# A gelu written out: tanh on the scalar engine, its argument and last factor on the vector engine

## The reference, cut to what matters

```
def peer_ffn(h, w_q, sub_keys, u_tab, v_tab):
    # q = h @ w_q; scores against the sub keys; top 16 of each half, top 16 of their sums
    cv, ci = lax.top_k(cand, 16)                  # for each token and each of 8 heads
    gates = jax.nn.softmax(cv, axis=-1)           # 128 factors a token
    def chunk_fn(xc, ic, gc):                     # 128 tokens
        uc, vc = take(u_tab, ic), take(v_tab, ic) # 128 rows of 1024 for each token
        act = jax.nn.gelu(einsum('cd,ckd->ck', xc, uc))   # the tanh form
        return einsum('ck,ckd->cd', gc * act, vc)
```

## Time and profile before

| | |
|---|---|
| median of 3 runs | 2805.45 us (2803.26 to 2807.54) |
| profiled execution, own time | 2803.49 us |
| its span on the core | 2801.3 us |
| busy: PE, DVE, ACT, POOL | 90%, 49%, 23%, 18% |
| chain that ended last, by engine | PE 55%, DMA 22%, DVE 9%, SP's queue 7%, ACT 5% |
| DVE line L1939, dots | 512 instructions, 612.1 us busy, 202.8 us idle before them |
| ACT line L1452, gelu | 256 instructions, 52.2 us; 52 table loads, 66.7 us |
| ACT line L1443, softmax exponentials | 31 table loads, 39.8 us |
| DVE line L1950, coefficients | 256 instructions, 56.0 us; 184.4 us idle before them |

### The profile page before, as it was taken

One profiled execution on the slowest core, in us unless ns is written; L12 is line 12 of the kernel. 1 busy time (PEld: TensorE's weight loads), 2 busy tenths in 40 slices (PEclk: granted clock), 3 DMA queues, 4 the chain that ended last, 5 costly groups with the idle time before them and its releaser, 6 DMA issues.

```text
span 2801.3 us, 31076 instructions
## 1 busy us (share of the span) xinstructions
PE 2531.6 (90%) x10682; PEld 1293.7 (46%) x10682; DVE 1365.7 (49%) x3708; ACT 643.4 (23%) x1475; POOL 494.7 (18%) x534
## 2 busy tenths in 40 slices
PE   9899999999999998998987889889899799798876
PEld 6644444443343343996443334336444346333332
DVE  2312222212212213556677776775675665678753
ACT  0310100101001001231222242442332542332212
POOL 1000000000000000002333332232322222333330
PEclk9989999999999999999999999999999999999999
DMA  7479999999999998458999999999999989999994
GB/s 248 195 295 415 418 416 418 419 416 418 418 417 418 419 417 332 151 211 325 420 421 421 421 419 384 419 368 418 420 418 417 408 334 418 406 398 422 422 421 168
DMA packets 179718, 1058.04 MB, mean 378 GB/s; under 512 B 18816, under 2 KB 19240, under 8 KB 81312
## 3 DMA queue, kind: packets, MB, share of 16 engines
q0 software_dynamic: 75104, 540.07, 47.1%
q1 hardware_dynamic: 104512, 516.71, 45.9%
HBM read 1055.64 MB, written 2.63 MB: 378 GB/s over the span
## 4 chain that ended last, share of the span: by engine, by line
PE 55%; DMA 22%; DVE 9%; SPq 7%; ACT 5%; issue 2%; POOL 0%; DVEq 0%; ACTq 0%; POOLq 0%
PE ps L1093 17%; DMA big<-in_uv,small 15%; PE ps L704 14%; DMA big<-in_w_gate_up 7%; PE ps L817 5%; SPq L434 4%; PE ps L694 3%; SPq L426 3%; PE ps L910 3%; DVE big L1939 3%; PE ps L1045 2%; PE ps L926 2%; PE ps L739 2%; PE ps L560 1%; ACT L1452 1%
## 5 line engine op out<-in xcount | busy, mean ns | idle before, releaser
L1093 PE MATMUL ps<-big,small 128*128 128x512 f32 x2048 | 993.8, 635 | 201.1 <-ACT small L1457 201.1
L2078 POOL DMA_INDIRECT big<-in_uv,small x512 | 484.1, 946 | 2209.1 <-DVE small L1919 1230.8
L1093 PEld LDWEIGHTS ps<-big,small 128*128 128x128 f32 x2048 | 401.4, 203 | 740.4 <-issue 452.2
L704 PE MATMUL ps<-big 128*64 128x512 f32 x3072 | 705.7, 601 | 22.8 <-DMA big<-in_w_gate_up 19.5
L1939 DVE SCALAR_TENSOR_TENSOR big<-big,ps 128x1024 f32<-128x1024 f32 x512 | 612.1, 1217 | 202.8 <-DMA big<-in_uv,small 202.6
L704 PEld LDWEIGHTS ps<-big 128*64 128x64 f32 x3072 | 203.6, 137 | 418.5 <-issue 337.9
L1457 ACT ACTIVATE small<-con,small 128x128 f32<-128x128 f32 x512 | 177.6, 394 | 311.1 <-DVE small L1950 309.2
L1687 DVE COPY big<-ps 128x512 f32<-128x512 f32 x32 | 22.1, 692 | 418.8 <-PE ps L704 418.8
L1673 DVE TENSOR_TENSOR big<-ps,big 128x256 f32<-128x256 f32 x64 | 27.2, 425 | 309.2 <-PE ps L721 309.2
L1452 ACT ACTIVATE small<-small 128x2 f32<-128x2 f32 x256 | 52.2, 204 | 528.5 <-DVE big L1939 520.7
L817 PEld LDWEIGHTS ps<-hT,ring 128*128 128x128 f32 x1280 | 146.2, 192 | 8.6 <-issue 7.2
(11 more groups left out here) (299 smaller groups left out, 1950.7 us busy)
## 6 DMA issues: line engine op xcount, KB each, us to landing
big<-in_w_gate_up SPq DMA_DIRECT2D x256, 1024.0 KB, 20.2
big<-in_w_down SPq DMA_DIRECT2D x128, 1024.0 KB, 23.1
ring<-in_peer_w_q SPq DMA_DIRECT2D x48, 512.0 KB
ring<-in_w_kv SPq DMA_DIRECT2D x22, 512.0 KB
ring<-in_w_in SPq DMA_DIRECT2D x16, 512.0 KB
ring<-in_a_w_in SPq DMA_DIRECT2D x16, 512.0 KB
big<-in_uv,small POOLq DMA_INDIRECT x512
ring<-in_ple_w_gate SPq DMA_DIRECT2D x16, 512.0 KB
```

The lines of the kernel that those rows point to most:

```text
L704: last = pe.matmul(ps[side * CAP:(side + 1) * CAP, bank + b, :], o, w[:, at:at + BANK], start=start, stop=stop, skip_group_check=True)
L1093: last = pe.matmul(ps[:, out_bank(f) + z, :], diagonal(k), rows(k)[:, D + z * BANK:D + (z + 1) * BANK], start=(k % PHASE == 0), stop=((k + ...
L2078: pool.indirect_dma_start(out=rows(k), out_offset=None, in_=io[f"uv{n // UNITS}"], in_offset=bass.IndirectOffsetOnAxis(ap=rows_at[:, at:at ...
```

## The change

The gelu's instruction on ACT becomes a tanh with scale sqrt(2/pi) on an argument that DVE prepares. DVE, after the two dots of the share, computes `g_cube` = 0.044715 d * d and `g_arg` = (g_cube + 1) * d, and signals `dots_ready` after that; for these it waits for its own dots. After `gelu_ready` it computes `g_twice` = (tanh + 1) * d and then the coefficient from it. The factor 0.5 goes into `p_rec`, in one more small instruction per head. Three small tiles are added in free columns of `small`; they aren't doubled, one set serves all shares. Nothing else changes, no transfer and no PE instruction.

```diff
--- before.py
+++ after.py
@@ -346,6 +346,7 @@
         pick = small[:, 784:912].bitcast(BF16)
         i12, e_row = small[:, 912:944], small[:, 944:960]
         p_sum, p_rec, p_nmax = (small[:, 960 + k * UNITS:960 + (k + 1) * UNITS] for k in range(3))
+        g_cube, g_arg, g_twice = (small[:, 1008 + k * SHARE:1008 + (k + 1) * SHARE] for k in range(3))
         cv = small[:, 1024:1024 + PICKS]
         rows_at = small[:, 1280:1280 + PICKS].bitcast(U32)
         dots, acts, coef = (small[:, 1536 + k * PICKS:1536 + (k + 1) * PICKS] for k in range(3))
@@ -1449,7 +1450,7 @@
                 k = n * SHARE
                 act.wait_ge(S["dots_ready"], n + 1)
                 at = slice(k % PICKS, k % PICKS + SHARE)
-                act.activation(acts[:, at], dots[:, at], ACT.Gelu_apprx_tanh).then_inc(S["gelu_ready"], 1)
+                act.activation(acts[:, at], g_arg, ACT.Tanh, scale=float(np.sqrt(2 / np.pi))).then_inc(S["gelu_ready"], 1)
                 act.wait_ge(S["coef_ready"], n + 1)
                 for k in range(n * SHARE, (n + 1) * SHARE):
                     if k >= DIAGS:
@@ -1938,16 +1939,21 @@
                     r = rows(k)[:, 0:D]
                     ins = dve.scalar_tensor_tensor(r, r, 1.0, tok, op0=ALU.mult, op1=ALU.mult,
                                                    accum_out=dots[:, k % PICKS:k % PICKS + 1])
-                ins.then_inc(S["dots_ready"], 1)
+                link(ins)
+                at = slice(n * SHARE % PICKS, n * SHARE % PICKS + SHARE)
+                link(dve.scalar_tensor_tensor(g_cube, dots[:, at], 0.044715, dots[:, at], op0=ALU.mult, op1=ALU.mult))
+                dve.scalar_tensor_tensor(g_arg, g_cube, 1.0, dots[:, at], op0=ALU.add, op1=ALU.mult)\
+                    .then_inc(S["dots_ready"], 1)
                 u16 = u % UNITS
                 if t % SHARES == 0:
                     dve.wait_ge(S["cv_exp"], u + 1)
                     link(dve.reciprocal(p_rec[:, u16:u16 + 1], p_sum[:, u16:u16 + 1]))
+                    link(dve.tensor_scalar(p_rec[:, u16:u16 + 1], p_rec[:, u16:u16 + 1], 0.5, None, ALU.mult))
                 for which, piece in chosen(f, t):
                     choose(which, piece)
-                at = slice(n * SHARE % PICKS, n * SHARE % PICKS + SHARE)
                 dve.wait_ge(S["gelu_ready"], n + 1)
-                dve.scalar_tensor_tensor(coef[:, at], acts[:, at], p_rec[:, u16:u16 + 1], cv[:, at],
+                link(dve.scalar_tensor_tensor(g_twice, acts[:, at], 1.0, dots[:, at], op0=ALU.add, op1=ALU.mult))
+                dve.scalar_tensor_tensor(coef[:, at], g_twice, p_rec[:, u16:u16 + 1], cv[:, at],
                                          op0=ALU.mult, op1=ALU.mult).then_inc(S["coef_ready"], 1)
 
             mask2 = triu.unsqueeze(1).broadcast_to((P, 4, P))
```

## The result

| | us, median | ratio, 95% interval |
|---|---|---|
| before (20 runs) | 2805.15 | |
| after (20 runs) | 2810.99 | 1.0023 (1.0017 to 1.0030) |

The change makes the kernel 5.8 us slower by the medians, 6.5 us (4.8 to 8.4) by the ratio, just more than the 0.2% that the prediction set as its bound. The profiled execution of after has a span of 2811.5 us against 2801.3, so the two traces differ by more than the medians do. The size of the whole change is taken from the medians, that of each experiment from its ratio; the traces are read for where things lie.

A forecast was written before the change was run, and what follows sets the result against it. DMA transfers were taken as the bound, with time to win or lose only in dips: first heads -4.1, second heads -2.9, last-phase start +3.1, tail +0.6, together -3.3 us, giving 2802.1 us against the median, range 2789 to 2814.

The forecast's parts named there:

- stretch C: Up to the third dip (2480 to 2510 us), at the change to the last phase: added DVE steps cost +3.1 us.
- the tail: End of the kernel: the last share is on the path, +0.6 us.
- full share: A share (two gathered rows) whose dots are on the path pays all three added DVE steps, 0.63 us.
- The load at 2486.82: Table load after a sigmoid in the last-phase dip: counted as 0 gained, 1.28 us as the other end.
- The drain: Skill page's further 1380 ns per table switch; not counted, since the chain's row shows 1.29 us in all.
- the heads' term: Attention heads of both token tiles, where transfers dip: loads removed (10.2 and 6.4 us) outweigh added DVE steps.
- short shares: Shares where DVE waits for ACT anyway pay only the second factor behind the tanh, 0.21 us.
- The loads' term: Thirteen table loads on the path in the two tiles' heads go, worth 10.2 and 6.4 us, 16.6 in all.
- The rest hidden: Outside the dips full transfers hide added DVE work; thinnest from 2500 to 2660 us, by 0.25 us a share.
- The list of dips: Where DMA engines are not full: 1820 to 1880 us (8.7 us), 2220 to 2300 (16.3), 2480 to 2510 (3.6).
- DVE as the bound: Rival, last phase: a share costs DVE more than the transfers' 4.98 us; time 2819, chance 0.17.
- The clock: Rival, head dips: shorter idles keep TensorE's clock up, giving back 12 us at most; 2796 at half, chance 0.22.

The follow-up runs named there:

- tanh_only: Kernel before with the gelu replaced by a tanh of the dots, nothing added on DVE; 2791.56 against 2803.78 us, ratio 0.9954.
- heads_only: Kernel before with the written-out gelu only in ticks 22 to 39 of phases 1 and 2, half in the identity; 2802.30 us, ratio 0.9995.
- tanh_heads: Kernel before with a plain tanh of the dots, no DVE steps, only in ticks 22 to 39 of phases 1 and 2; 2793.56 us, ratio 0.9963.
- dve_only: Changed kernel with the gelu back on ACT and all of DVE's added steps kept; 2820.88 us, ratio 1.0056 to the kernel before.
- last_only: Kernel before with the written-out gelu only in the last phase (f = 3), half in the identity; 2808.03 against 2803.78 us, ratio 1.0011.
- first_only: Kernel before with the written-out gelu only in phase 0, half in the identity; 2805.21 us, ratio 1.0002.
- rest_only: Kernel before with the written-out gelu in phase 0 and in phases 1 and 2 outside ticks 22 to 39; 2807.53 us, ratio 1.0013.
- mixed: Tanh throughout, argument on ACT in ticks with search work and no logarithm, otherwise on DVE with last product beside the tanh; 2804.43 us, ratio 1.0001 to before.
- heads_mixed: Kernel before with that mixed form only in ticks 22 to 39 of phases 1 and 2; 2800.53 us, ratio 0.9989.
- all_shadow: Changed kernel with the dots' product made during the tanh and the half in the identity; 2804.86 us, ratio 1.0004 to the kernel before.

## Why the prediction was wrong, point by point

- **The direction.** Forecast were 3.3 us less, measured were 5.8 more. The time lies in the range (2789 to 2814), but the sign is wrong. Of the rivals none came as written. Of the 9.1 us between the two, 7.1 are in the heads and 2.1 in the part held to be hidden; stretch C and the tail came 0.6 under the sum.
- **Prices.** A step of 0.21 us (measured 0.20), a full share of 0.63 (0.59), the tanh at the gelu's 204 ns, at least 60 loads gone (66 at these two lines, 10 more at the chain's exponentials): right. "Below 0.17 nothing small lies" was a misreading: before has 32 steps of 128x1 at L1900, of 0.154 us each, and the new ones take 0.154 to 0.164; it changes nothing, since a linked step counts by its 0.20 us. The load at 2486.82, counted as 0 gained, does go: in after the sigmoid at 2494.70 and the tanh at 2495.67 have no load between them. That is the 1.28 us held open for stretch C, and with it the forecast would have been further off, at -4.6 us. The drain of the Trainium skill ("ScalarE: Activation LUTs", section "What ACT_TABLE_LOAD costs") would have given more gain than the rows; tanh_only gave less, so it has no support here.
- **The failed step: the heads' term, that what DVE and ACT gain or lose there "counts in full", counted on the chain of before.** The sum had -8.5 us (8.1 of steps less 16.6 of loads); heads_only measured -1.4 (-3.9 to +1.1). It keeps the first exponential's load as tanh_heads does, which is 1.3 us of the miss. The traces show where it went, by the start of the coefficients' step (us) of the same share:

| share | before | tanh_heads | heads_only | dve_only | after |
|---|---|---|---|---|---|
| phase 1, tick 22 | 1774.72 | 1776.58 | 1776.03 | 1779.13 | 1779.51 |
| phase 2, tick 0 | 2024.79 | 2020.05 | 2025.59 | 2035.62 | 2028.18 |
| phase 2, tick 20 | 2158.45 | 2154.47 | 2159.15 | 2168.87 | 2160.79 |
| phase 2, tick 63 | 2437.54 | 2427.94 | 2438.48 | 2455.53 | 2444.05 |

From tick 22 to the end of phase 1, and from tick 20 to the end of phase 2, tanh_heads takes 6.6 and 5.6 us less than before, heads_only 0.5 less and 0.2 more, dve_only 6.4 and 7.6 more. These are single executions; where last_only and first_only have no edit, the same spans differ from before by up to 1.5 us. So the loads gave about 12 us (10.4 by the times) where 15.3 of the sum were tested, and the steps of dve_only cost 14 where the sum had 4.6 and 3.5. (dve_only has its steps in the ticks outside the heads as well; rest_only, which has only those, takes 0.6 us more in the two spans together.) By the times alone, tanh_heads against heads_only, the steps cost 9.0 us and some 4 either way, which does not exclude 8.1. How the rest of the miss divides between loads and steps is therefore not settled; that each was read too favourably is what the traces say.

The chain by line from tick 22 to tick 54 of phase 1, before (1774 to 1974 us) and then in dve_only (1779 to 1984 us), shows where the steps' cost comes from:

```profile
by line: PE ps L1093 37.6%; PE ps L1045 14.3%; PE ps L910 7.0%; DVE big L1939 5.7%; issue 4.8%; ACT L1452 4.1%; ACT small L1457 1.9%; ACT L1403 1.9%; ACT L1443 1.3%; ACT big L1399 1.3%; ACT big L1400 1.3%; DVE small L1950 1.1%; ACT big L139
```

```profile
by line: PE ps L1094 24.8%; PE ps L1046 13.9%; DVE big L1940 12.3%; PE ps L911 5.1%; issue 5.0%; ACT L1453 4.2%; ACT L1404 1.9%; DVE small L1956 1.7%; ACT small L1458 1.7%; DVE big L2030 1.3%; DVE small L1955 1.3%; DVE small L1914 1.3%; DVE
```

All loads are still there, and the path has gone over from PE's diagonals (37.6 to 24.8%) to DVE's dots (5.7 to 12.3%). In the first heads the loads' going pushes the path the same way (tanh_heads above, 12.7 to 25.4%). The changed kernel has both. Its chain between 2186 and 2300 us, where the sum had four full and four short shares, 3.5 us, by line and then at the steps L1944 (a full share) and L1955 of the short ones:

```profile
by line: DMA big<-in_uv,small 23.6%; DVE big L1940 23.2%; PE ps L1094 8.7%; issue 7.2%; DVE big L2036 4.3%; ACT L1453 3.4%; DVE big L2028 3.0%; ACT big L1400 2.8%; ACT big L1401 2.8%; ACT big L1404 2.5%; DVE small L1956 2.5%; ACT big L1399 
...
2191.12 0.17 DVE small L1944
...
2199.34 0.17 DVE small L1944
...
2202.70 0.17 DVE small L1944
...
2210.91 0.17 DVE small L1944
...
2219.61 0.17 DVE small L1955
...
2234.17 0.17 DVE small L1944
...
2245.49 0.17 DVE small L1955
...
2250.69 0.17 DVE small L1944
...
2257.70 0.17 DVE small L1944
...
2262.18 0.17 DVE small L1944
...
2272.23 0.17 DVE small L1955
...
2277.43 0.17 DVE small L1944
...
2280.79 0.17 DVE small L1944
...
2287.89 0.17 DVE small L1944
...
2291.25 0.17 DVE small L1944
```

Twelve full and three short: 12 x 0.59 + 3 x 0.20 = 7.7 us. DVE's dots are 23% of this chain and were 7% of it before (above). Counted in the same way, the first heads of after (1784 to 1885 us) have eleven full and four short shares, 7.3 us against 4.6 in the sum. The 15.0 us together are near the 14 of dve_only. The reading that fits: the path through PE and ACT and the path through DVE are nearly equally long in the heads, and the chain names only one of them. Many shares that the chain of before left out or had as short became full ones as soon as DVE had more to do, with the loads or without them. This is read off the chains; no run varies DVE's work in small amounts to show where the path changes.
- **The loads' term** was too high for two reasons that the traces of tanh_heads show: in the first heads the transfers are full again, and in the second PE takes over. "The savings can't exceed the dips, and they don't" holds for the net saving, not for the loads alone (10.2 us against 8.7 in the first heads).
- **Stretch C and the tail** (+3.7 us): last_only measured +3.1 (0.6 to 5.6), with the sigmoid's load gone too. Right, though the steps alone may be dearer by that load's 1.3 us.
- **The rest hidden.** Right for phase 0 (+0.6 us). Elsewhere a term was probably missing: rest_only measured +3.6 us (1.4 to 6.2) where the sum had 1.5. The list of dips left out 1700 to 1740 us, where before was at 358 GB/s and after at 324. PE is the bound there (busy 40.00 of 40 us before, 38.68 after); the steps ahead of it make it start late. Between ticks 6 and 12 of phase 1 after falls back by 3.1 us in its trace.
- **DVE as the bound** came in part, after the third dip, at the 3 us that stretch C held anyway. **The clock** came back in the first heads (0.91 to 0.97 in 1820 to 1880 us) but not in the second (0.91, now 0.92). No run separates what that gave.
- **What stays open:** how the miss in the heads divides, and why the argument on ACT gains nothing in ticks where DVE has search work to hide it (mixed, heads_mixed). ACT's longer work lies beside search work there, so it should cost nothing; no run tells whether PE or the diagonals behind it are next.

## What to carry to other kernels

When an edit takes work from one engine on the path and gives work to another, do not price both on the chain of before: where two paths are nearly equally long, added work counts in shares that the chain does not name, and removed work stops counting when the next engine takes over. Ask which engine is next. A better count for the steps is not shown: the chain of tanh_heads has fourteen full and seven short shares in the two heads, 9.7 us, and the measured 9.0, some 4 either way, fits that as well as the sum's 8.1. What can be had is a run of each part alone (here 12.9 us of gain and 15.7 of cost). An edit that pays in two short stretches only should be made in these only. Work that prepares for the far side of a wait (the product that doesn't need the tanh) belongs in front of it: all_shadow is 4.7 us better than the change.

## What the runs showed of the hardware

Fewer loads were left than one for each change of function. The exponential's line has one load of 31, as expected, since it shares the tanh's table. At the tanh's line 16 are left, where ten square roots, eight logarithms and four sigmoids in front would make 22. Eight stand behind a square root and eight behind a logarithm, none behind a sigmoid: three times a tanh follows a sigmoid with no load between (2494.70 and 2495.67 us in after), so the sigmoid's table serves the tanh. The gelu's does too: in tanh_heads the tanh at 1776.26 us, the first after the gelus, has no load, and the exponential at 1785.60 us needs one (1784.30), where in the changed kernel the chain's exponential L1400 needs none. A 128x1 activation whose scale and bias are read from a tile takes 379 ns, where the 128x2 one with an immediate takes 204.
